# First layer of a three-layer transformer kernel: layer input brought in transposed, row norm applied when results leave PSUM

## The reference, cut to what matters

```python
h = _rmsnorm(x, ln_mix_g[l])          # x * rsqrt(mean(x*x)+EPS) * gain, per token
proj = h @ w_in[l]                    # 1024 -> 7748 columns
(aq, ak, av, iq, ik, iw, hq, hf, hi, hg, cb, cc, ch, gates) = _split_cols(proj)
q = _rmsnorm(aq ...); k = _rmsnorm(ak ...)
y_attn = _dsa_attention(q, k, v, iq ..., ik, iw, rel_bias)   # index scores, top 64 keys, softmax
o = _hgrn2(hq ..., hf ..., hi ..., lb_all[l])                # gated linear recurrence
y_conv = cb * _short_conv(cc * ch, conv_w[l])
g = jax.nn.sigmoid(gates ...)
```

## Time and profile before

| | |
|---|---|
| median of the runs | 1130.84 us |
| the profiled execution, first to last instruction (span) | 1129.4 us |
| instructions | 18037 |
| TensorE matmul busy | 97% of the span |
| VectorE / ScalarE / GpSimd busy | 59% / 50% / 1% |
| mean granted TensorE clock | 0.993 |
| moved from memory | 182.5 MB |

### The profile page before, as it was taken

One profiled execution on the slowest core, in us unless ns is written; L12 is line 12 of the kernel. 1 busy time (PEld: TensorE's weight loads), 2 busy tenths in 40 slices (PEclk: granted clock), 3 DMA queues, 4 the chain that ended last, 5 costly groups with the idle time before them and its releaser, 6 DMA issues.

```text
span 1129.4 us, 18037 instructions
## 1 busy us (share of the span) xinstructions
PE 1099.5 (97%) x6800; PEld 970.6 (86%) x6800; DVE 667.6 (59%) x978; ACT 567.3 (50%) x803; POOL 10.3 (1%) x15
## 2 busy tenths in 40 slices
PE   6999999999999999999999999999999999999996
PEld 5989877887998999897887999988987789989995
DVE  5796696757655545645455655465654656465543
ACT  6645645755554445523545644454545755454441
POOL 0010010000000000000000000000000000000000
PEclk9999999999999999989999999999999999999999
DMA  7754333465555655443323466546442424656530
GB/s 283 260 169 149 113 131 131 160 213 168 171 183 190 210 194 187 154 144 128 112 97 113 171 208 205 180 160 216 155 152 83 129 77 165 206 185 213 197 130 37
DMA packets 52601, 184.38 MB, mean 163 GB/s; under 512 B 5816, under 2 KB 8128, under 8 KB 52544
## 3 DMA queue, kind: packets, MB, share of 16 engines
q1 hardware_dynamic: 51488, 182.53, 47.7%
q10 hardware_dynamic: 1056, 1.06, 0.3%
HBM read 182.50 MB, written 1.06 MB: 163 GB/s over the span
## 4 chain that ended last, share of the span: by engine, by line
PE 86%; DVE 9%; ACT 2%; DMA 1%; issue 1%; DVEq 0%; SPq 0%; ACTq 0%
PE ps L377 25%; PE ps L378 25%; PE ps L379 25%; PE ps L446 3%; DVE wlo L1352 3%; PE ps L495 2%; PE ps L519 2%; DMA raw<-stream 1%; DVE hT_lo L1372 1%; DVE arena L1461 1%; PE ps L570 0%; DVE stat L1460 0%; ACT whi L954 0%; PE ps L841 0%; PE ps L586 0%
## 5 line engine op out<-in xcount | busy, mean ns | idle before, releaser
L1352 DVE TENSOR_TENSOR wlo<-raw,whi 128x1024 fp32r<-128x1024 f32 x339 | 405.6, 1222 | 192.5 <-ACT whi L954 191.0
L954 ACT ACTIVATE whi<-raw 128x1024 fp32r<-128x1024 f32 x339 | 348.1, 1053 | 195.3 <-PE ps L379 132.7
L377 PE MATMUL ps<-hT_hi,whi 128*128 128x256 f32 x1144 | 328.3, 287 | 0.2
L378 PE MATMUL ps<-hT_lo,whi 128*128 128x256 f32 x1144 | 324.6, 284 | 0.0
L379 PE MATMUL ps<-hT_hi,wlo 128*128 128x256 f32 x1144 | 324.6, 284 | 0.0
L377 PEld LDWEIGHTS ps<-hT_hi,whi 128*128 128x128 f32 x1144 | 220.3, 193 | 2.7 <-DVE hT_lo L1372 1.1
L378 PEld LDWEIGHTS ps<-hT_lo,whi 128*128 128x128 f32 x1144 | 220.5, 193 | 1.0 <-issue 0.2
L379 PEld LDWEIGHTS ps<-hT_hi,wlo 128*128 128x128 f32 x1144 | 220.4, 193 | 0.0
L377 PE MATMUL ps<-whi,y_hi 128*128 128x512 f32 (+1 forms) x540 | 213.7, 396 | 2.6 <-DVE y_lo L1439 2.0
L378 PE MATMUL ps<-wlo,y_hi 128*128 128x512 f32 (+1 forms) x540 | 209.9, 389 | 0.0
L379 PE MATMUL ps<-whi,y_lo 128*128 128x512 f32 (+1 forms) x540 | 209.8, 389 | 0.0
(11 more groups left out here) (221 smaller groups left out, 785.3 us busy)
## 6 DMA issues: line engine op xcount, KB each, us to landing
raw<-stream SPq DMA_DIRECT2D x339, 512.0 KB, 4.2
x<-x_in SPq DMA_DIRECT2D x2, 512.0 KB, 3.8
arena<-scratch ACTq DMA_DIRECT2D x1, 1024.0 KB, 11.2
arena<-rb SPq DMA_DIRECT2D x1, 1024.0 KB, 7.0
out<-x SPq DMA_DIRECT2D x4, 256.0 KB, 2.1
cst<-const SPq DMA_DIRECT2D x1, 906.0 KB, 8.8
arena<-gfin SPq DMA_DIRECT2D x1, 512.0 KB, 7.1
sml<-small SPq DMA_DIRECT2D x1, 101.5 KB, 3.9
```

What stands on the lines that cost most here:

```text
L377: pe.matmul(o, a[0], b[0], start=start, stop=False)
L378: pe.matmul(o, a[0], b[1], start=False, stop=False)
L954: act.activation(whi[:, u % RING, :], raw[:, u % RAW, :], ACT.Copy).then_inc(sem("hi_done"), 1)
L1352: dve.tensor_tensor(wlo[:, u % RING, :], raw[:, u % RAW, :], whi[:, u % RING, :].bitcast(F32), ALU.subtract).then_inc(sem("lo_done"), 1)
```

## The change

A second input `xt_in` is x transposed on the host, [128, 8, 256]. Hence:

- ScalarE's queue issues `small` (gains) and four DMAs of `xt_in` before anything else. SyncE's queue issues unit 0, unit 1, x, unit 2, identity, unit 3, then units 4 to 7, and only then the large constants.
- `hi_first` and `lo_first` split xT times gain straight from SBUF, interleaved with hi and lo of units 0 to 3. Squares of x and the norm factor follow after that; `nrs` is its negative.
- The scaled copy of x and the 16 transposes go.
- After unit 5 TensorE spreads `rs` (`spread_rs(0)`), VectorE keeps it (`keep_rsB(0)`, step 5).
- The F jobs iqk, hf, hq, cc, ch, cb leave PSUM through VectorE (`evac_v`, at steps 10, 14, 18, 26, 30, 34) instead of ScalarE. The T jobs leave through ScalarE in two scaled instructions instead of one.
- The t5 table moves from unit 3 to unit 6, its read-back from step 6 to step 9.

```diff
@@ sync engine
-            for t in range(TT):
-                sp.dma_start(x[:, t, :], x_in[t * P:(t + 1) * P, :]).then_inc(sem(f"x_in{t}"), 16)
-            sp.dma_start(cst[:, 0:P], const[:, 0:P]).then_inc(sem("id_in"), 16)
-            sp.dma_start(sml[:], small).then_inc(sem("id_in"), 16)
...
-            for u in range(RAW):
-                load(u, u)
+            load(0, 0)
+            load(1, 1)
+            for t in range(TT):
+                sp.dma_start(x[:, t, :], x_in[t * P:(t + 1) * P, :]).then_inc(sem(f"x_in{t}"), 16)
+            load(2, 2)
+            sp.dma_start(cst[:, 0:P], const[:, 0:P]).then_inc(sem("id_in"), 16)
+            load(3, 3)
+            for u in range(RAW, 2 * RAW):
+                sp.wait_ge(sem("lo_done"), u - RAW + 1)
+                load(u % RAW, u)
             sp.dma_start(cst[:, P:N_CONST], const[:, P:N_CONST]).then_inc(sem("c_in"), 16)
@@ tensor engine
-            pe.wait_ge(sem("id_in"), 32)
-            norm(0)
...
-                if u == 3:
+                if u == 5:
+                    pe.wait_ge(sem("id_in"), 16)
+                    spread_rs(0)
+                if u == 6:
                     pe.wait_ge(sem("c_in"), 16)
...
                 if u == 11:
-                    pe.wait_ge(sem("evac"), evac_no["iqk"] + 1)
+                    pe.wait_ge(sem("evac_v"), evac_v_no["iqk"])
@@ scalar engine
+            def hi_first(b):
+                act.wait_ge(sem(f"xt_in{b}"), 16)
+                for k in (2 * b, 2 * b + 1):
+                    m = act.activation(hT[0][:, k, :], xT[:, k, :], ACT.Copy, scale=sml[:, G_MIX + k:G_MIX + k + 1])
+                m.then_inc(sem("n_hi"), 1)
...
+            act.dma_start(sml[:], small).then_inc(sem("sml_in"), 16)
+            for b in range(4):
+                act.dma_start(xT[:, 2 * b:2 * b + 2, :], xt_in[:, 2 * b:2 * b + 2, :]).then_inc(sem(f"xt_in{b}"), 16)
             act.preload_act_table_set("natural_log_exp_and_others")
+            hi(0)
+            act.wait_ge(sem("sml_in"), 16)
+            for b in range(4):
+                hi_first(b)
+                if b < 3:
+                    hi(b + 1)
             for t in range(TT):
...
             rsqrt(rs, nt, "n_v", 1, "n_r")
-            for u in range(2):
-                hi(u)
-            for b in range(4):
-                hi_x(0, b)
-            for u in range(2, LEAD):
+            for u in range(4, LEAD):
                 hi(u)
...
-                if u == 3:
+                if u == 6:
                     act.wait_ge(sem("t5_ps"), 1)
...
-                if u == 6:
+                if u == 9:
@@ vector engine
+            def lo_first(b):
+                dve.wait_ge(sem("n_hi"), b + 1)
+                for k in (2 * b, 2 * b + 1):
+                    m = dve.scalar_tensor_tensor(hT[1][:, k, :], xT[:, k, :], sml[:, G_MIX + k:G_MIX + k + 1],
+                                                 hT[0][:, k, :].bitcast(F32), ALU.mult, ALU.subtract)
+                m.then_inc(sem("n_lo"), 1)
+
+            dve.memset(bias1, 1.0)
+            for b in range(4):
+                lo(b)
+                lo_first(b)
             dve.wait_ge(sem("n_ss"), TT)
...
             refine(rs, nt, tmp2)
-            for t in range(TT):
-                dve.tensor_scalar(x_n[:, t, :], x[:, t, :], rs[:, t:t + 1], None, ALU.mult).then_inc(sem("n_x"), 1)
-            dve.memset(bias1, 1.0)
-            lo(0)
-            for b in range(4):
-                lo_x(0, b)
-            for u in range(1, LEAD):
+            dve.tensor_scalar(nrs, rs, -1.0, None, ALU.mult).then_inc(sem("n_rs"), 1)
+            for u in range(4, LEAD):
                 lo(u)
...
+            FIRST = {10: ("iqk", iqk), 14: ("hf", hz), 18: ("hq", hqf), 26: ("cc", ccT), 30: ("ch", chT), 34: ("cb", cbT)}
...
+                if u == 5:
+                    keep_rsB(0)
+                if u in FIRST:
+                    evac_v(*FIRST[u], 1.0, 0)
```

86 lines of the change are left out of this document (39 added, 47 removed).

## The result

The changed kernel takes 1136.55 us in the median of 4 runs (1134.3 to 1137.3), the kernel before 1131.15 beside it: ratio 1.0048, 95% interval 1.0034 to 1.0062. It is slower by 5.4 us. The forecast was 1131.8 with a range up to 1134.6, so the result lies outside it, on the slower side.

> The changed kernel itself, unchanged, in the same shared rounds, for more of its times and clocks. Theory: median 1134.5 to 1136.5, and each run's time less 1130 x (1 - its granted clock) at 1125.5 to 1126.5, against 1123 to 1124.5 for the kernel before.

The account below looks back on a forecast made before the run. TensorE, doing matmuls for 97% of the span, was taken as the bound, losing time only where it stands still. Terms -0.6 + 2.3 - 1.2 + 0.4 = +0.9 on 1130.84 gave about 1131.8 us, range 1128.6 to 1134.6.

Parts of the forecast that it names:

- The three places: Where TensorE waits: the start, after unit 10 for VectorE's norm, after unit 23 until the mask releases the first attention step.
- Term 1: Start to unit 11: hi(13) starts at 33.6 against 34.22, so -0.6 us, bounds 0 and -3.2.
- its own case: The prediction's main case, all terms as taken: about 1131.8 us, 1130.3 to 1133.1 by its bounds, chance 0.5.
- Term 2: Stretch to unit 23: copies of hf and hq added on VectorE, 1.14 each, +2.3 us, covered by nothing.
- Term 3: At the mask: its instructions no longer meet GpSimd, 0.4 lost at lo(27); -1.2 us, bounds 0 and -1.6.
- Term 4: T jobs leaving in two instructions, with TensorE behind such a copy at hg and the first gate: +0.4 us, 0 to +0.8.
- cc, ch and cb at 0: Attention steps: these VectorE copies, 1.14 each, taken to cost nothing; +3.4 us were each passed on to TensorE.
- The early start: Rival: TensorE's earlier start survives, Term 1 is -3.2 to -4; 1128.7 us, down to 1128.3; chance 0.2.
- The slower rival: VectorE's copies delay attention steps, Term 1 and Term 3 are 0; 1134.6 us, 1135.7 with two steps; chance 0.2.
- Copies partly hidden: Rival: TensorE's products ahead of the mask set the pace, Term 2 is 1; 1130.4 us; chance 0.1.
- The signs: Expected trace times: unit 0's matmul near 8 us, lo(4) near 21, transposes after unit 10 near 43, first attention step near 88.

Follow-up runs that it names:

- hold_start: Changed kernel with TensorE's unit 0 held back until `lo_first(1)` is done; 1136.45 us, ratio 1.0048 to the kernel before.
- const_mid: Changed kernel with the 906 KB of constants issued between the loads of units 5 and 6; 1134.23 us, ratio 1.0029 to the kernel before.
- norm_first: Changed kernel with the query and key norm ahead of lo(13) and lo(14) in VectorE's order; 1132.25 us, ratio 1.0003 to the kernel before.
- before_two: Kernel before with two unread 128x1024 VectorE instructions added at steps 14 and 18; 1133.12 us, ratio 1.0022 to the kernel before.
- late_mul: Changed kernel with hf and hq copied unscaled by ScalarE and multiplied on VectorE at steps 24 and 25; 1133.28 us, ratio 1.0046.
- keep_busy: Changed kernel with 22 unread matmuls on TensorE between unit 10 and its wait; 1134.40 us, ratio 1.0030 to the kernel before.
- sq_late: Changed kernel with x's squares and norm factor ahead of `hi_first(2)`, and hf and hq multiplied on VectorE at steps 24 and 25; 1135.05 us, ratio 1.0036.
- all_four: Changed kernel with early squares, hf and hq multiplied at steps 24 and 25, t5 copy one step later, constants between loads 5 and 6; 1131.28 us, ratio 1.0004.

## Why the prediction was wrong

**What bounds the kernel: right.** The three places were the right ones, in the right order, and each named the engine that still releases TensorE: VectorE's norm after unit 10, and L1569 (L1557 before) at the mask. That an early start of TensorE alone does not move unit 11 is what happened, and `hold_start` shows it from the other side.

**Term 1 (-0.6) failed: it was +1.7.** The chain that it counts is the right chain; its numbers were too early, one after another. The five DMA issues on ScalarE's queue took 3.1 us (0.74 to 3.87) where I had 2.15, and unit 0 was used at 5.44 and not 4.4. Unit 2 was used at 13.63 and not 12.2, in part because less was moved in these 9 us than I assumed:

```profile
4.00:13.00 9.00, 3.31 (x8) 2.64 (x9) 4.21 (x6) 4.99 (x7) 0.00 (x0) 1.00 1.02 384
```

That is 384 GB/s at full DMA share, where rows 3 have 402. On the 3.3 MB from 4 us to unit 2 this is 0.4 us of the 1.4; the rest no row here tells apart. Unit 0's piece was split at 9.6 and not 8.1. The squares therefore came at 17.15 (15.9), and lo(4) ended at 22.20 (21.2). Unit 8's load was then behind 906 KB of constants, issued at 18.27 and landing 6.6 us later, and was used 4.5 us after its issue at 22.38, not 3.5: hi(8) at 26.92 (24.8). From there the count held: hi(13) 9.0 behind hi(8) where I had 8.8. So the error is 2.1 us at hi(8), half from the start and half from a load that I priced near the lowest landing time of the rows (3.4) and not at their median (4.5), with constants standing before it. In `const_mid`, without them, hi(8) came at 25.73. The range for term 1 went from -3.2 to 0. Its upper bound was the real mistake: it had no room for a loss, though I had written that lo(4), which asks for unit 8, comes 1.5 us later. The bounds of its terms also do not give the 1130.3 to 1133.1 that it names for its own case: added up they give 1128.3 to 1133.9, so the result lay above even these.

**And what that lateness meets.** The prediction named lo(13) as the start of the VectorE work but took the order as given. It had TensorE 3 us ahead at unit 10; it was 1.0 ahead at that unit's end (42.23 against 43.25). Unit 0 took 4.4 us where it took 3.7, the t5 table was now made behind unit 6, and unit 7 waited 1.02 for the copy of job aq (the row at 30.45). That 1.0 of lead, the 0.3 that it waited before and the 1.7 by which the transposes are late make the 3.05 of standing still. In the changed kernel that is where unit 11 and the clock are lost, and `norm_first` gives both back; but the same edit gains 1.3 us of schedule time in the kernel before, so that not all of its worth is a repair of the change.

**Term 2 (+2.3): right,** 1.14 twice, seen also in `before_two`. **Term 3 (-1.2): right in kind,** -1.4 measured (0.85 and 0.72 on the mask, less 0.14). The price I subtracted for lo(27) was 0.14 and not 0.4 (the row at 82.75, 1.37 instead of 1.23). MAX8 and MATCH_REPLACE8 ran beside GpSimd at their usual lengths (0.43 and 0.41 at 81.76 and 82.30, inside its 80.80 to 83.03). The Trainium skill, "SBUF — State Buffer", section "SBUF: two separate sides", gave the rule that instructions in a two-port mode or with two SBUF inputs contend for the shared ports and others do not. The traces agree in all three kinds. Top-8, with one input, passes. The mask's second instruction has two inputs; beside GpSimd it is held (1.01, L1549 before and L1566 in `late_mul`), and clear of it it takes 0.29 (L1561). The mask's first has one input and is held too (1.20 against 0.35); its 384 elements in 0.35, against 128 in 0.29 for L1561, fit the two-port mode, which no row names. **Term 4 (+0.4): right,** +0.27. **cc, ch and cb at 0: right,** the shift of TensorE is 4.08 at unit 25 and at unit 38; it passes through.

**What the sum had no term for is the clock.** It is 2 to 2.7 us of the loss: 1130 x (0.9938 - 0.9914) = 2.7, up to 0.8 of it from the half clock behind the last matmul. I assumed one mean clock for both kernels, as the two profiled executions happen to have. Without the wait after unit 10 (`norm_first`) it is all back; with the wait filled (`keep_busy`) most of it is, as far as runs of different rounds can tell.

**The rivals.** The early start did not survive. The slower rival (1134.6 to 1135.7) came near the time for another reason: no attention step from 91 to 135 us waits for VectorE in the changed kernel. Its mechanism is real, as `late_mul`, `sq_late` and `all_four` show at unit 28, with 0.86 for one step. "Copies partly hidden" was not the case.

**The signs.** First matmul at 9.7 (8 forecast), lo(4) at 22.2 (21), transposes at 45.3 (43) and waiting for VectorE, two copies of 1.14 in their place, short mask instructions, first attention step at 89.9 (88). All of the right kind, all late by 1.2 to 2.3 us.

## What to carry to other kernels

An engine's lead is worth only what the next engine to release it can follow: before starting the bound engine earlier, go along the order of the one that releases it next and ask what stands there ahead of the work that is needed, and whether it needs to. Here one reordering on VectorE was worth nearly as much as the whole loss, while four well-founded repairs, each alone, were worth 1 us of schedule time or less. Give the kernel before the same repair, too: part of its worth was a gain that needed no change. When a step that issues loads comes later, price its load as landing behind whatever was issued ahead of it, and give that term an upper bound above zero. And on a kernel that is bound by TensorE at full clock, a new wait of some 3 us may cost some 2 us more through the granted clock; compare means over ten executions, since a single profiled one may show none of it.
